# Two transformer-like layers on one core: weight remainders placed between convolution steps, norm roots by token tile, a last FF block by tile

## The reference, cut to what matters

```python
h = rms_norm(x, ffn1_pre_g)
x = x + 0.5 * rms_norm(swiglu(h, w_gate, w_up, w_down), ffn1_post_g)      # D_FF = 2816
h = rms_norm(x, mix_pre_g)
q, k, v, z, xbc, dt = split(h @ w_in)
xbc = silu(causal_depthwise_conv(xbc, conv_w, conv_b))                    # 1536 channels, 4 taps
mixed = concat([diff_attention(q, k, v), ssd(z, xbc, dt)]) @ w_out
x = x + rms_norm(mixed, mix_post_g)
x = x + 0.5 * rms_norm(swiglu(rms_norm(x, ffn2_pre_g), ...), ffn2_post_g)
```

## Time and profile before

| | us |
|---|---|
| median of 3 runs | 1616.08 (1614.79 to 1616.84) |
| the profiled execution | 1617.17 |
| its span, first to last instruction | 1615.4 |
| TensorE busy (PE) | 1563.2 |
| VectorE busy (DVE) | 1256.4 |
| ScalarE busy (ACT) | 800.3 |

### The profile page before, as it was taken

One profiled execution on the slowest core, in us unless ns is written; L12 is line 12 of the kernel. 1 busy time (PEld: TensorE's weight loads), 2 busy tenths in 40 slices (PEclk: granted clock), 3 DMA queues, 4 the chain that ended last, 5 costly groups with the idle time before them and its releaser, 6 DMA issues.

```text
span 1615.4 us, 26273 instructions
## 1 busy us (share of the span) xinstructions
PE 1563.2 (97%) x9128; PEld 1357.2 (84%) x9128; DVE 1256.4 (78%) x2158; ACT 800.3 (50%) x1216; POOL 105.5 (7%) x68
## 2 busy tenths in 40 slices
PE   8999899999999999999999999999997999999998
PEld 7888798899998888888888888788886877778886
DVE  5575679999998777677777777888886887688877
ACT  5544445467775333444444444644445564454443
POOL 0000177700000000000000000000000000000000
PEclk9999999999999999999999999999999999999999
DMA  6544344533325555555555555455553423345552
GB/s 225 192 157 176 137 156 158 182 131 105 129 105 184 201 186 194 196 182 182 185 197 189 182 190 198 172 206 192 191 182 117 155 82 130 130 150 201 182 185 101
DMA packets 39386, 270.43 MB, mean 167 GB/s; under 512 B 4881, under 2 KB 5393, under 8 KB 7074
## 3 DMA queue, kind: packets, MB, share of 16 engines
q1 hardware_dynamic: 37440, 266.45, 46.3%
q10 hardware_dynamic: 1890, 3.24, 0.6%
HBM read 268.62 MB, written 1.05 MB: 167 GB/s over the span
## 4 chain that ended last, share of the span: by engine, by line
PE 78%; DVE 15%; issue 3%; ACT 2%; DVEq 1%; DMA 0%; SPq 0%; ACTq 0%
PE ps L702 50%; PE ps L735 16%; PE ps L737 7%; DVE wlo L550 3%; DVE wlo L2041 2%; DVE raw L2012 2%; PE ps L734 1%; PE ps L688 1%; DVE arena L2275 1%; DVE wlo L2012 1%; DVE whi L2012 1%; ACT whi L529 1%; DVE XT L1774 1%; DVE arena L2348 0%; PE ps L954 0%
## 5 line engine op out<-in xcount | busy, mean ns | idle before, releaser
L735 PE MATMUL ps<-XT,whi 128*128 128x512 f32 x1200 | 429.9, 398 | 0.8 <-DVE wlo L550 0.4
L702 PE MATMUL ps<-XT,whi 128*128 128x256 f32 x1696 | 313.0, 299 | 10.4 <-DVE wlo L550 10.3
L737 PE MATMUL ps<-XT,wlo 128*128 128x256 f32 x1050 | 294.9, 281 | 0.0
L529 ACT ACTIVATE whi<-raw 128x1024 fp32r<-128x1024 f32 x182 | 191.2, 1058 | 171.4 <-PE ps L702 142.1
L702 PE MATMUL ps<-whi,HAh 128*128 128x512 f32 x696 | 272.4, 391 | 3.0 <-DVE HAl L2182 2.0
L702 PEld LDWEIGHTS ps<-XT,whi 128*128 128x128 f32 x1696 | 265.1, 194 | 12.0 <-issue 9.8
L702 PE MATMUL ps<-wlo,HAh 128*128 128x512 f32 x696 | 271.2, 390 | 0.0
L702 PE MATMUL ps<-whi,HAl 128*128 128x512 f32 x696 | 270.8, 389 | 0.0
L735 PEld LDWEIGHTS ps<-XT,whi 128*128 128x128 f32 x1200 | 223.0, 189 | 46.3 <-DVE wlo L550 0.6
L550 DVE TENSOR_TENSOR wlo<-raw,whi 128x1024 fp32r<-128x1024 f32 x162 | 196.2, 1222 | 78.2 <-ACT whi L529 76.7
L737 PEld LDWEIGHTS ps<-XT,wlo 128*128 128x128 f32 x1050 | 198.8, 189 | 5.8
(11 more groups left out here) (285 smaller groups left out, 2077.2 us busy)
## 6 DMA issues: line engine op xcount, KB each, us to landing
raw<-in_experts SPq DMA_DIRECT2D x128, 1024.0 KB, 4.7
raw<-in_panels SPq DMA_DIRECT2D x58, 1024.0 KB, 4.8
raw<-in_ffa SPq DMA_DIRECT2D x33, 1024.0 KB, 4.7
raw<-in_ffb SPq DMA_DIRECT2D x33, 1024.0 KB, 4.7
arena<-in_row_post ACTq DMA_DIRECT2D x3, 512.0 KB, 3.8
X<-in_x SPq DMA_DIRECT2D x2, 512.0 KB, 5.3
arena<-in_row_ln ACTq DMA_DIRECT2D x2, 256.0 KB, 3.7
arena<-in_row_post SPq DMA_DIRECT2D x1, 512.0 KB, 5.6
```

What stands on the lines that cost most here:

```text
L529: act.activation(whi[:, buf(p), :], half(item_of(p), p % 2), ACT.Copy).then_inc(part_hi, 1)
L702: last = pe.matmul(out, x if w_moving else w, w if w_moving else x, start=start and n == 0, stop=stop and n == 2)
L735: last = pe.matmul(out, wh[:, k], XT[:, k], start=k == 0, stop=k == NK - 1)
L737: pe.matmul(out[:, T:], wl[:, k], XTh[:, k], start=False, stop=False)
```

## The change

- *Convolution.* VectorE writes remainder S_XB+2j+4 between `conv_rows(j)` and `conv(j)` and S_XB+2j+5 behind `conv(j)`; the taps of blocks 0 and 1 come ahead of the dt and lambda operations. On ScalarE the rounding of S_XB+2j+4 stands ahead of the first taps of block j. The semaphore `xraw_in` gives way to the bank's own read count.
- *Norms behind products* (4, 6, 8) and the second norm of the first layer (1). VectorE turns the sum of a tile's first quarter into `sum / D + eps` (`tile_mean`); ScalarE takes the root of the second quarter's sum with that as its bias, one root per token tile (`tile_root`), and VectorE one reciprocal per tile (`tile_scale`). Norm 1 has four squares of 512 columns in place of two of 1024. The order of products and updates in `post_norm` is interleaved.
- *One part split ahead.* Ahead of the norm at the end of the experts, of the first FF and of the output projection one part is prepared in place of two; the second comes between norm and stream, or behind the stream.
- *End of the FFs.* The last block's hidden values are made per token tile (`last_times_up`), and TensorE's last down part waits for each tile by itself.

```diff
@@ TensorE, feed_forward
-                down(NF - 1, s0 + 3 * NF - 1, s0 + 3 * NF, 1, stop=True)
+                pe.wait_ge(part_lo, s0 + 3 * NF)
+                for tt, (done, n) in enumerate(((fa_first, 2 if base else 1), (fa_ready, NF + fb))):
+                    pe.wait_ge(done, n)
+                    for ins in v_part([bank(name) for name in outs], s0 + 3 * NF - 1, hidden_acts(1), False, True,
+                                      (2 * tt, 2 * tt + 1)):
+                        ins.then_inc(main_done, 1)
@@ ScalarE
+            def tile_root(i, tt, done):
+                act.wait_ge(norm_ms, NORM_MEANS[i] + tt + 1)
+                act.wait_ge(norm_sq, sum(NORM_PARTS[:i]) + done)
+                act.activation(nst[:, i % 2, 6 + tt:7 + tt], nst[:, i % 2, 2 * tt + 1:2 * tt + 2], ACT.Sqrt,
+                               scale=1.0 / (D * NORM_GAIN.get(i, 1.0) ** 2),
+                               bias=nst[:, i % 2, 4 + tt:5 + tt]).then_inc(norm_sd, 1)
+            def tile_stats(i, parts, arrive):
+                squares = SQUARES[i % 2].rearrange("p t d -> p (t d)")
+                for n, part in enumerate(parts):
+                    arrive[n]()
+                    act.activation(squares[:, 512 * n:512 * n + 512], part, ACT.Square,
+                                   accum_out=nst[:, i % 2, n:n + 1]).then_inc(norm_sq, 1)
+                    if n == 2:
+                        tile_root(i, 0, 3)
+                tile_root(i, 1, 4)
@@ norm 1
-            split_to(S_WQ + 1)
+            split_to(S_WO + 5)
+            warm_root(4)
             tiles = [X[:, tt, :] for tt in range(NT)]
-            warm_root(4)
-            norm_stats(1, tiles, [lambda: read_out(act, "ho2"), lambda: read_out(act, "ho3")])
+            squares = XN.rearrange("p t d -> p (t d)")
+            for hf in range(2):
+                for tt in range(NT):
+                    n = 2 * tt + hf
+                    if hf:
+                        split_to(S_WQ + tt)
+                    read_out(act, f"ho{2 * hf + tt}")
+                    act.activation(squares[:, 512 * n:512 * n + 512], X[:, tt, 512 * hf:512 * hf + 512], ACT.Square,
+                                   accum_out=nst[:, 1, n:n + 1]).then_inc(norm_sq, 1)
+            for tt in range(NT):
+                tile_root(1, tt, 3 + tt)
@@ experts to the first FF
+            split_to(S_FFA)
+            warm_root(1)
             split_to(S_FFA + 1)
-            warm_root(1)
             stream_hi("ffa")
@@ end of the first FF (the output projection's end has the same with S_FFB)
                 if not base:
-                    split_to(S_MIX + 1)
+                    split_to(S_MIX)
...
-            norm_stats(4, *products_of("fa"))
+            tile_stats(4, *products_of("fa"))
+            split_to(S_MIX + 1)
             stream_hi("mix")
@@ conv_first
-                split_to(limit(USE_PART[f"xb{j}"]))
-                act.wait_ge(xraw_in, j + 1)
+                split_to(S_XB + 2 * j + 4)
+                read_out(act, f"xb{j}")
@@ VectorE, post_norm
+                tile_mean(i, 0, 1)
+                gained(0)
+                gained(1)
+                tile_mean(i, 1, 3)
+                gained(2)
+                tile_scale(i, 0)
+                piece(0)
+                if pieces == "by tokens":
+                    piece(1)
+                    gained(3)
+                    tile_scale(i, 1)
+                    piece(2)
+                    piece(3)
+                    return
+                tile_scale(i, 1)
+                piece(2)
+                gained(3)
+                piece(1)
+                piece(3)
@@ experts to the first FF
-            split_to(S_FFA + 1)
+            split_to(S_FFA)
...
+            split_to(S_FFA + 1)
             stream_lo("ffa")
@@ last_times_up
+                    first, second = slice(0, P), slice(P, T)
+                    link(dve.tensor_tensor(HAf[:, first], HID[:, b, first], HAf[:, first], ALU.mult))
+                    link(dve.tensor_copy(HAh[:, b, first], HAf[:, first]))
+                    dve.tensor_tensor(HAl[:, b, first], HAf[:, first], HAh[:, b, first].bitcast(f32), ALU.subtract)\
+                       .then_inc(fa_first, 1)
...
@@ convolution
             conv_rows(0)
+            conv(0)
             split_to(S_XB + 5)
+            conv_rows(1)
+            conv(1)
+            split_to(S_XB + 7)
             dve.wait_ge(dt_ln, 1)
...
-            conv(0)
-            for j in range(1, 6):
+            for j in range(2, 6):
                 conv_rows(j)
                 conv(j)
+                split_to(S_XB + 2 * j + 5)
```

More of the change, by code:

```diff
@@ L219 @@
 T_PART = {"n1": -3, "ya": S_WA - 9, "yb": S_WA, "mg": S_WO - 1, "n2": S_WQ - 1, "idx": S_G - 2,
-          "ffa": S_FFA - 1, "mix": S_MIX - 1, "dtt": S_MIX + 1, "xs": S_AK - 1, "bm": S_AK - 1, "pt": S_WM - 1, "att": S_WM - 1,
-          "ssm": S_WM + 2, "ffb": S_FFB - 1}
+          "ffa": S_FFA - 2, "mix": S_MIX - 2, "dtt": S_MIX + 1, "xs": S_AK - 1, "bm": S_AK - 1, "pt": S_WM - 1, "att": S_WM - 1,
+          "ssm": S_WM + 2, "ffb": S_FFB - 2}
 TSTAGES = [("n1", 4), ("ya", 2), ("yb", 2), ("mg", 4), ("n2", 4), ("idx", 2), ("ffa", 4), ("mix", 4),
@@ L846, in _ @@
             pe.wait_ge(gla_l, 1)
-            pe.wait_ge(pool_const, 12)
+            pe.wait_ge(pool_const, 11)
             for tt in range(NT):
@@ L1521, in feed_forward @@
                 if not base:
-                    split_to(S_MIX + 1)
+                    split_to(S_MIX)
             feed_forward(S_FFA, 0)
             products_of = lambda name: ([bank(f"{name}{i}") for i in range(4)],
-                                        [lambda i=i: take(f"{name}{i}") for i in range(4)])
+                                        [lambda i=i: arrived(act, f"{name}{i}") for i in range(4)])
             warm_root(2)
-            norm_stats(4, *products_of("fa"))
+            tile_stats(4, *products_of("fa"))
+            split_to(S_MIX + 1)
             stream_hi("mix")
@@ L1636, in _ @@
             stream_hi("ssm")
-            norm_stats(6, *products_of("wm"))
+            split_to(S_FFB)
+            tile_stats(6, *products_of("wm"))
+            split_to(S_FFB + 1)
             stream_hi("ffb")
@@ L1691, in read_done, with tile_mean @@
                 ins.then_inc(main_read["dve"], 1)
-            def norm_join(i):
-                dve.wait_ge(norm_sq, sum(NORM_PARTS[:i + 1]))
-                halves = nst[:, i % 2, 0:4].rearrange("p (t h) -> p t h", t=2)
-                dve.tensor_tensor(nst[:, i % 2, 4:6], halves[:, :, 0], halves[:, :, 1], ALU.add).then_inc(norm_ms, 1)
+            def tile_mean(i, tt, done):
+                dve.wait_ge(norm_sq, sum(NORM_PARTS[:i]) + done)
+                g2 = NORM_GAIN.get(i, 1.0) ** 2
+                dve.tensor_scalar(nst[:, i % 2, 4 + tt:5 + tt], nst[:, i % 2, 2 * tt:2 * tt + 1], 1.0 / (D * g2), EPS / g2,
+                                  ALU.mult, ALU.add).then_inc(norm_ms, 1)
@@ L1699, in norm_root, with tile_scale @@
+            def tile_scale(i, tt):
+                dve.wait_ge(norm_sd, NORM_ROOTS[i] + tt + 1)
+                link(dve.reciprocal(nst[:, i % 2, 8 + tt:9 + tt], nst[:, i % 2, 6 + tt:7 + tt]))
             def norm_root(i):
-                dve.wait_ge(norm_sd, i + 1)
+                dve.wait_ge(norm_sd, NORM_ROOTS[i] + 1)
                 link(dve.reciprocal(nst[:, i % 2, 8:10], nst[:, i % 2, 6:8]))
-            def pre_norm(i, dst):
-                norm_root(i)
-                for tt in range(NT):
-                    src = X[:, tt, :] if i != 1 else ident[:, :]
-                    last = dve.tensor_scalar(dst[:, tt, :], src, nst[:, i % 2, 8 + tt:9 + tt], None, ALU.mult)
-                    last.then_inc(norm_out, 1)
@@ L1711, in post_norm, with gained @@
-            def post_norm(i, names, loads, pieces=None):
+            def post_norm(i, names, loads, pieces):
                 dve.wait_ge(post_in, 16 * loads)
-                for n, name in enumerate(names):
+                def gained(n):
                     tt, hf = n // 2, n % 2
-                    take(name)
+                    dve.wait_ge(main_done, MAIN_AT[names[n]] + 1)
                     dve.wait_ge(norm_sq, sum(NORM_PARTS[:i]) + n + 1)
-                    if n == len(names) - 1:
-                        norm_join(i)
-                    read_done(dve.tensor_tensor(XN2[:, tt, 512 * hf:512 * hf + 512], bank(name),
+                    read_done(dve.tensor_tensor(XN2[:, tt, 512 * hf:512 * hf + 512], bank(names[n]),
@@ L1731, in post_norm, with piece @@
[L1731 to L1739 removed]
+                def piece(n):
+                    tt, hf = n // 2, n % 2
+                    c = slice(512 * hf, 512 * hf + 512)
+                    read_out(dve, names[n])
+                    dve.scalar_tensor_tensor(X[:, tt, c], XN2[:, tt, c], nst[:, i % 2, 8 + tt:9 + tt], X[:, tt, c],
+                                             ALU.mult, ALU.add).then_inc(x_piece, 1)
@@ L1914, in _ @@
```

(12 more changed lines are left out.)

85 lines of the change are left out of this document (41 added, 44 removed).

## The result

The changed kernel takes 1604.84 us (median of 4 runs, 1603.46 to 1606.44), the kernel before 1616.46 beside it; ratio 0.9925, 95% interval 0.9913 to 0.9937: 0.75% faster. A second comparison, of five runs, gave 1603.35 (1601.68 to 1604.18) and a ratio of 0.9911 (0.9898 to 0.9925). The profiled execution took 1603.59 us.

What follows compares the result with a forecast made beforehand. TensorE bounds the kernel, busy 1563.2 of 1615.4 us; VectorE paces the convolution stage. Terms 10.9 + 0.5 + 0.75 + 0.3 + 0.45 + 0.3 = 13.2 us off, from median 1616.08 to 1602.9; range 1599.5 to 1607.

Steps and rivals of the forecast that it cites:

- Convolution, 10.9: Convolution stage: blocks of 5.61 us on VectorE, under TensorE's 5.76, gain 10.9 us; bounds 8.5 and 11.7.
- one pause at part 9: Convolution stage: TensorE still waits 0.8 us for remainder 9, whose ScalarE rounding stands behind the first Silu and table load.
- The rival of 0.20: Attention stage: VectorE's backlog or late ScalarE rounding gives back 2 to 5 us, 1604.5 to 1608; chance 0.20.
- Mix norm, 0.5: Norm after the first FF: VectorE's stream of remainders begins earlier, 0.5 us gained; bounds -0.5 and 1.5.
- FF-b norm, 0.75: Norm behind the output projection: products and first update come earlier, the stream's wait goes, 0.75 us gained; bounds 0 and 1.2.
- Second norm, 0.3: Second norm of the first block: TensorE's 3.03 us pause shrinks by 0.3 us; bounds 0 and 0.6.
- Experts' end, 0.45: First FF's transposes: VectorE's adds no longer wait for remainder S_FFA+1, 0.45 us gained; bounds 0 and 0.9.
- The end, 0.3: Kernel's end: last updates begin 0.35 earlier, pay 0.35, lose the joint wait for squares: 0.3 us; bounds -0.3 and 0.6.
- the clock stays up: Long norms and second norm: shorter pauses no longer drop the clock, 2.6 us more gained, 1600.3 us; chance 0.22.

Runs made afterwards that it cites:

- the experiment: The changed kernel with the last hidden block of both feed-forwards in one piece again, TensorE waiting once for it: 1601.70 us, one profile.
- convolution edit alone: The kernel before with only the convolution's lines of the change, norms and feed-forward ends as before: 1605.47 us, ratio 0.9921.
- the best version: The changed kernel with the four dt and lambda operations behind the last convolution block and unread matmuls at seven pauses: 1601.29 us, ratio 0.9900.

## Why the prediction was right, step by step

- **Convolution, 10.9.** Measured 10.92 and 10.84. The steps behind it hold: block 5.69 (said 5.61, under 5.76), taps without a wait, part 15 ahead by what was said, one pause at part 9. That pause is 0.51, costing 0.67, for a stated 0.8, but the reason given was a part only: ScalarE's rounding behind the table load is worth 0.2 of it, while moving VectorE's four small operations, which hold up both engines, removes all of it. The 1.28 of the row was the right price for the load (here too, 1250.09 to 1251.38, the Silu starts 0.01 after it). By the drain that the Trainium skill adds (ScalarE: Activation LUTs, What ACT_TABLE_LOAD costs) the stage would have given 9.5; the trace does not agree, since no gap stands on either side of this load.
- **Nothing lost in attention.** 93.95 and 93.89 us. The rival of 0.20 did not come. (Its times should read 1604.9 to 1607.9, by 2 to 5 us on 1602.9.)
- **Mix norm, 0.5.** 244.38 - 243.76 = 0.62, and 233.46 - 232.92 = 0.54. Its pause is 2.36, said 2.7. Of its parts the earlier release of TensorE gives nothing there, as the experiment shows; the others (the freed remainder, the order of the updates, the small operations) were not taken apart.
- **FF-b norm, 0.75.** The term that was mis-sized, in both directions. With the same falls of the clock (convolution edit alone against after) column E goes from 208.88 to 208.30, and 0.3 of that is the split block: about 0.3 for the norm. The step that failed is the remainder S_FFB+1, moved behind the stream, of which the prediction said that it is there in time with nothing to spare. Count from the last row of the output projection, 1405.05 in the edit alone and 1402.56 after. The row at 1411.49 comes 8.93 us on, in the edit alone 9.67 (1414.72): 0.74 gained, near the 0.75 that was forecast. Two rows on TensorE waits for that remainder, 0.17 shown, and behind the wait only 0.28 of the 0.74 is left. The edit alone has no wait there. A kernel with the remainder elsewhere was not run. Besides, in both profiles of the kernel before the clock was low for 3.4 us of lost work behind this norm, where the changed kernel has 1.7 or none, and that adds 1.07 (209.95 against 208.88). So 0.3 or 1.3. Why the kernel before has more half clock there is not shown.
- **Second norm, 0.3.** The pause fell by 0.50, column A by 0.48 (190.57 to 190.09, both with one fall) and 0.46 (192.22 to 191.76). Said too low.
- **Experts' end, 0.45.** 352.83 - 352.48 = 0.35.
- **The end, 0.3.** The earlier release gives it (pause 0.99 to 0.67, counted in column E). Column F is flat, so the two other parts of this term, the small operations and the joint wait, came to nothing together.
- **The sum.** With equal clock 10.9 + 0.6 + 0.3 + 0.5 + 0.35 + 0.3 = 12.95, said 13.2: 0.45 too much at FF-b and 0.2 too little at the second norm cancel in part, which is luck. The spans differ by 13.6, because in after the half clock at f costs 1.07 less, a fall at a costs 0.65 that the kernel before did not have, and the first row of column A starts 0.18 earlier.
- **The clock.** The rival "the clock stays up" came true in part, and its prices were near: 1.6 said and 1.6 measured at the second norm (190.09 against 188.49), 0.7 said and 0.6 to 0.75 at the mix norm, 0.3 said and nothing at FF-b. With the pause of 3.03 the clock fell at the second norm in 3 of 3 profiles; with 2.53 in 3 of 8 (those without unread matmuls). At FF-b (1.85) it fell in 6 of 8, at the mix norm (2.36) always. The Trainium skill, TensorE: Matmul & The Clock Gate, The HAM clock gate, says that the gate's phase runs free of the kernel; the traces agree in that the same pause of the same code brought a fall in some executions and none in others.
- **The time.** 1602.9 was said, 1604.84 and 1603.35 measured. The profiled execution (said 1604.0, was 1603.59) was close, partly by the same luck; that the median lies 1.09 below it was not so. In the profiled executions the falls at a, n and t cost 0.5 to 1.7 us each; for the others their mean clock alone speaks.

## What to carry to other kernels

When two engines take turns inside a block (VectorE writes the rows, ScalarE the first tap, VectorE the other taps), put independent work of the right length into the gap: here 1.13 us into a wait of 1.16, six times, was worth 7 us. When an operation is split so that another engine starts earlier, count what it adds to its own engine's queue: where that engine sets the next step the split is lost (first FF), where it only waits it is won (second FF). Before comparing two executions of a kernel with pauses of 1.5 to 3 us on TensorE, list the stretches of low granted clock in both; here they made 1.7 to 2.5 us between profiled executions of identical code, as much as five of the six edits together. And when a piece of work is moved out of a pause, look for the next place that needs it: at the FF-b norm 0.46 of 0.74 us went back there.

## What was not expected of the hardware

- In fourteen profiles a fall of the granted clock took up to 1.7 us of work wherever it came (up to 3.4 at c in the three profiles with the old convolution, and at f in the two of the kernel before); at a it showed as 0.5 us in the time where part of it lay in a pause (191.02 against 190.57; 0.65 by 190.74 against 190.09) and as 1.6 where it lay on matmuls (192.22 against 190.57).
- It comes or stays away with identical code: behind the pauses at 165 to 169 in 7 of 13 profiles, behind the one of 1.52 at the output projection in 3 of 12.
- Matmuls that nobody reads hold it at 1.00: eleven pauses were filled in three kernels (n, m and f of each, t in two) and no fall stood behind any; unfilled, with the same norms, n had one in 3 of 8 profiles, m in 8 of 8, f in 6 of 8. For n and t alone, where a fall is the exception, three and two profiles would not show it. Where they stand beside the pause instead of in it, they cost about what they take: 1.06 us for ten records in the best version (0.11 each).
